# First modulation by channel chunks and eight tiles multiplied as chunks come, in a two-block fp32 transformer kernel

## What is computed

```
mod   = silu(c)     @ ada_w + ada_b        # 1024 -> 6 * 1024
mod_c = silu(c_ctx) @ ada_w + ada_b
sh1, sc1, g1, sh2, sc2, g2 = split(mod, 6);  sh1c, sc1c, ... = split(mod_c, 6)
h  = rms_norm(x,   norm1_w) * (1 + sc1)  + sh1      # 512 tokens
hc = rms_norm(ctx, norm1_w) * (1 + sc1c) + sh1c     # 256 context tokens
p  = h @ w_in                                       # q, k, v, z, xs, b, c, dt
kc, vc, xs_c, b_c = parts of hc @ w_in
```

## Time and profile before

| | us |
|---|---|
| median of 3 runs | 1377.66 |
| lowest, highest | 1375.05, 1383.27 |
| the profiled execution | 1382.15 |
| its span | 1380.4 |
| busy in the span: PE, weight loads, VectorE, ACT, GpSimd | 1320.3, 1068.9, 573.1, 601.8, 619.4 |

### The profile page before, as it was taken

One profiled execution on the slowest core, in us unless ns is written; L12 is line 12 of the kernel. 1 busy time (PEld: TensorE's weight loads), 2 busy tenths in 40 slices (PEclk: granted clock), 3 DMA queues, 4 the chain that ended last, 5 costly groups with the idle time before them and its releaser, 6 DMA issues.

```text
span 1380.4 us, 17922 instructions
## 1 busy us (share of the span) xinstructions
PE 1320.3 (96%) x6626; PEld 1068.9 (77%) x6626; DVE 573.1 (42%) x1123; ACT 601.8 (44%) x937; POOL 619.4 (45%) x507
## 2 busy tenths in 40 slices
PE   8999999998898999999999989999989999999998
PEld 1787878777777788888888778766868888888886
DVE  2577544778446344444522371686330000001123
ACT  3722545874436344443322464687353323223231
POOL 0234334347623544444565734344614444444562
PEclk9999999999999999999999989999999999999999
DMA  9427454040131544545322412110303222232221
GB/s 392 164 101 267 165 163 96 32 153 1 62 122 57 217 182 182 190 190 216 149 108 94 166 61 86 37 47 32 122 18 104 91 91 91 94 109 102 92 92 61
DMA packets 27036, 165.60 MB, mean 120 GB/s; under 512 B 2736, under 2 KB 5040, under 8 KB 8544
## 3 DMA queue, kind: packets, MB, share of 16 engines
q1 hardware_dynamic: 24960, 150.11, 30.3%
q10 hardware_dynamic: 2016, 14.68, 2.9%
HBM read 162.65 MB, written 6.32 MB: 122 GB/s over the span
## 4 chain that ended last, share of the span: by engine, by line
PE 81%; DVE 6%; ACT 4%; POOL 4%; DMA 3%; issue 2%; SPq 0%; ACTq 0%; DVEq 0%; POOLq 0%
PE bank L272 52%; PE bank L331 12%; PE bank L308 6%; DMA ada_ring<-ada_dram 2%; POOL arena L921 2%; PE bank L686 1%; DVE ada_ring L1937 1%; PE bank L1307 1%; PE bank L1279 1%; DMA w_raw<-w_dram 1%; PE bank L525 1%; PE bank L513 1%; POOL arena L923 1%; DVE arena L2002 1%; PE bank L662 1%
## 5 line engine op out<-in xcount | busy, mean ns | idle before, releaser
L265 POOL TENSOR_TENSOR w_lo<-w_raw,w_hi 128x512 fp32r<-128x512 f32 x340 | 462.8, 1393 | 609.7 <-ACT w_hi L256 609.7
L272 PE MATMUL bank<-h_hi,w_hi 128*128 128x512 f32 x1120 | 441.9, 395 | 11.5 <-DVE h_lo L447 6.6
L272 PE MATMUL bank<-h_lo,w_hi 128*128 128x512 f32 x1120 | 438.5, 392 | 0.0
L272 PE MATMUL bank<-h_hi,w_lo 128*128 128x512 f32 x1120 | 438.2, 391 | 0.0
L256 ACT ACTIVATE w_hi<-w_raw 128x2048 fp32r<-128x2048 f32 x88 | 168.6, 1916 | 299.9 <-PE bank L272 176.5
L272 PEld LDWEIGHTS bank<-h_hi,w_hi 128*128 128x128 f32 x1120 | 211.8, 189 | 56.1 <-issue 7.4
L272 PEld LDWEIGHTS bank<-h_hi,w_lo 128*128 128x128 f32 x1120 | 211.9, 189 | 44.8
L272 PEld LDWEIGHTS bank<-h_lo,w_hi 128*128 128x128 f32 x1120 | 212.1, 189 | 42.9
L2266 DVE TENSOR_TENSOR arena<-arena,bank 128x512 f32 (+1 forms) x22 | 15.1, 688 | 209.3 <-PE bank L272 209.3
L2128 DVE TENSOR_TENSOR h_lo<-arena,h_hi 128x1024 fp32r<-128x1024 f32 x22 | 32.4, 1487 | 135.0 <-ACT h_hi L1763 123.5
L1956 DVE SCALAR_TENSOR_TENSOR arena<-bank,params,arena 128x511 f32<-128x511 f32 (+1 forms) x36 | 25.4, 705 | 136.6 <-ACT arena L1743 114.4
(11 more groups left out here) (272 smaller groups left out, 1854.0 us busy)
## 6 DMA issues: line engine op xcount, KB each, us to landing
w_raw<-w_dram SPq DMA_DIRECT2D x92, 1024.0 KB, 4.8
ada_ring<-ada_dram SPq DMA_DIRECT2D x30, 1024.0 KB, 4.8
ada_ring<-ada_dram ACTq DMA_DIRECT2D x14, 1024.0 KB, 5.0
arena<-ada_dram SPq DMA_DIRECT2D x4, 1024.0 KB, 10.7
arena<-x_dram SPq DMA_DIRECT2D x2, 2048.0 KB, 11.6
bias_copies<-bias_rows SPq DMA_DIRECT2D x1, 4096.0 KB, 17.4
arena<-bias_copies SPq DMA_DIRECT2D x4, 768.0 KB, 5.8
out_dram<-arena SPq DMA_DIRECT2D x8, 256.0 KB, 2.1
```

The costliest lines, as they stand in the source:

```text
L265: last = nc.gpsimd.tensor_tensor(w_lo[b % 2][:, part], w_raw[b % 2][:, part], w_hi[b % 2][:, part], ALU.subtract)
L272: last = nc.tensor.matmul(bank[:, :], w[:, ft, k, :], x[:, k, :], start=k == first and m == 0, stop=k == final and m == 2)
```

## The change

The modulation for shift and scale is now made by chunks of 128 channels, and the products start as chunks come.

- `ada1`'s first eight blocks are cut by output channel. Chunks 0 to 3 stay row products on PE (`ada_row_sums`: eight matmuls of 256 columns, 32 output rows each, into four groups of 32 partitions of bank 5; ACT copies the bank; `ada_columns` sums and turns the four groups with a matrix of ones and zeros, `pick`). Chunks 4 to 7 are transposed blocks, and VectorE makes the dots (`lead_dots`), for c and for c_ctx apart.
- PE sums the squares of x itself (32 mean matmuls); VectorE's sums of squares for x and ctx are gone, the latter replaced by one reduction.
- v comes before k in `KINDS`. The first eight tiles (blocks 0 to 3) go to eight banks, `X_BANK`. PE goes through chunks for blocks 0 and 1, then 2, and block 3 at the end; blocks 2 and 3 have their halves in arena space. The context of these eight tiles comes behind all eight, two tiles to a bank.
- v's banks are emptied by ACT between the context's affines; k's ropes stand on VectorE behind the copies of the first four contexts.
- The 16 other modulation blocks: 8 and 9 behind the ropes, then two per tile in n = 8 to 14; ACT issues both loads at the end of its turn n.

The diff, cut to its core:

```diff
-KINDS = [("k", j) for j in range(4)] + [("v", j) for j in range(4)] + [("xs", j) for j in range(4)] \
+KINDS = [("v", j) for j in range(4)] + [("k", j) for j in range(4)] + [("xs", j) for j in range(4)] \
...
+N_LEAD, N_ROW = 8, 4
+DOTS = [(4, 0), (5, 0), (4, 1), (6, 0), (7, 0), (5, 1), (6, 1), (7, 1)]
...
         def load_ada(eng, src, c, off=0):
 
-            eng.wait_ge(ada_used, c - 1 + off)
+            if c < 10:
+                eng.wait_ge(dots_done, N_DOT)
+            else:
+                eng.wait_ge(ada_used, c - 9 + off)
...
+        X_BANK = [0, 1, 2, 3, 6, 7, 4, 5]
...
+            sp.dma_start(con[:], T["con"]).then_inc(con_in, 16)
             load_block(sp, 0)
+            for k in range(4):
+                sp.dma_start(X[:, 2 * k:2 * k + 2, :], T["x"].rearrange("p (c n) -> p c n", c=DC)[:, 2 * k:2 * k + 2, :]).then_inc(x_in[k], 16)
+            load_lead(0)
             load_block(sp, 1)
+            load_lead(1)
+            load_lead(2)
+            load_block(sp, 2)
+            load_lead(3)
+            load_lead(4)
+            sp.dma_start(HC, T["ctx"].rearrange("p (c n) -> p c n", c=DC)).then_inc(ctx_in, 16)
+            for c in range(5, DC):
+                sp.wait_ge(rows_done, c - 4)
+                load_lead(c)
+            load_block(sp, 3)
...
+            def ada_row_sums(c):
+                pe.wait_ge(row_in[c], 16)
+                slab = lead_slot[c].rearrange("p f d -> p (f d)").rearrange("p (k n) -> p k n", k=DC)
+                for k in range(DC):
+                    g = slice(32 * (k % 4), 32 * (k % 4) + 32)
+                    last = nc.tensor.matmul(ps[5][g, 0:256], silu_pad[:, k, :], slab[:, k, :], start=k < 4, stop=k >= 4)
+                last.then_inc(rows_done, 1)
...
+            ada_row_sums(0)
+            ada_columns(0)
+            pe.wait_ge(row1_out, 4)
+            lead_products(0, (0,))
+            ada_row_sums(1)
+            ada_columns(1)
+            lead_products(0, (1,))
+            ada_row_sums(2)
+            ada_columns(2)
+            lead_products(0, (2,))
+            lead_products(1, (0,))
+            ada_row_sums(3)
+            lead_products(1, (1,))
+            ada_columns(3)
+            lead_products(1, (2,))
+            for b in (0, 1):
+                lead_products(b, (3,))
+            lead_products(2, (0, 1, 2, 3))
+            for k in (4, 5, 6, 7):
+                for b in (0, 1, 2):
+                    lead_products(b, (k,))
...
+            pe.wait_ge(lo_done, 4)
+            for ft in (0, 1):
+                if ft == 1:
+                    pe.wait_ge(hctx_scaled, 1)
+                for k in range(DC):
+                    last = chunk_products(3, ft, ps[X_BANK[6 + ft]], k)
+                last.then_inc(half_used, 1)
...
             for n, (kind, j) in enumerate(KINDS):
-                if n == 5:
-                    load_ada(act, T["ada1"][10], 10)
-                if 5 <= n < 15:
-                    c = 2 * n + 1 if n < 9 else n + 9
-                    load_ada(act, T["ada1"][c], c)
...
-                if 5 <= n < 8:
-                    load_ada(act, T["ada1"][2 * n + 2], 2 * n + 2)
+                if N_LEAD <= n < 15:
+                    load_ada(act, T["ada1"][2 * n - 6], 2 * n - 6)
+                    load_ada(act, T["ada1"][2 * n - 5], 2 * n - 5)
...
+            lead_low(3)
+            dve.wait_ge(row1_out, 4)
+            lead_dots(4, 0)
+            lead_xn(5)
+            lead_dots(5, 0)
+            lead_xn(6)
+            lead_low(4)
+            lead_dots(4, 1)
+            lead_xn(7)
+            lead_low(5)
+            lead_dots(6, 0)
+            dve.wait_ge(sq_done, 16)
+            nc.vector.tensor_reduce(ctx_sum, ctx_sq.rearrange("p c n -> p n c"), AX_X, ALU.add).then_inc(sq_used, 8)
+            lead_dots(7, 0)
+            lead_low(6)
+            lead_dots(5, 1)
+            lead_low(7)
+            scale_of(dve, 1)
+            lead_dots(6, 1)
+            dve.wait_ge(scale_out, 2)
+            nc.vector.tensor_tensor(HC, HC, ps[5][:, 0:CTX].unsqueeze(1).to_broadcast([P, DC, CTX]), ALU.mult).then_inc(hctx_scaled, 1)
+            lead_dots(7, 1)
...
+            dve.wait_ge(ctx_done, 4)
+            for n in range(4):
+                nc.vector.tensor_copy(vcT[:, n, :], lead_ctx(n)).then_inc(ctx_free, 1)
+            for n in range(4, N_LEAD):
+                dve.wait_ge(half_used, n + 1)
+                dve.wait_ge(tile_free, n)
+                rope(ps[X_BANK[n]], kT[:, n - 4, :], 1.0)
...
-                if 4 <= n < 8:
-                    add_ada1(2 * n)
-                    add_ada1(2 * n + 1)
-                if 8 <= n < 16:
-                    add_ada1(n + 8)
+                if N_LEAD <= n < 15:
+                    add_ada1(2 * n - 6)
+                    add_ada1(2 * n - 5)
```

More of the change, by code:

```diff
@@ L56 @@
 CCOL, _at = {}, 0
-for _n, _w in [("ident", 128), ("trif", 128), ("trib", 128), ("ones", 128), ("mean", 128), ("mean512", 128), ("eps", 1), ("epseps", 1)]:
+for _n, _w in [("ident", 128), ("trif", 128), ("trib", 128), ("ones", 128), ("mean", 128), ("mean512", 128), ("eps", 1), ("epseps", 1), ("pick", 2)]:
     CCOL[_n] = (_at, _w)
@@ L373, in add_squares @@
                 nc.vector.tensor_tensor(s, s, buf[:, k % 2, 0:n], ALU.add).then_inc(sq_used, 1)
-        def mean(pe, r, buf, bank, n=S):
-            pe.wait_ge(sq_used, 8 * r + 8)
-            s = buf[:, 2, 0:n] if r != 1 else tmp[:, 3, 0:n]
-            for t in range(n // P):
-                last = nc.tensor.matmul(ps[bank][:, t:t + 1], s[:, t * P:(t + 1) * P], con_("mean")[:, 0:1], start=True, stop=True)
-            last.then_inc(mean_done, 1)
         def mean_head(pe, r, buf, bank):
@@ new lines, in _ @@
+            for k in range(DC):
+                pe.wait_ge(sq_done, 2 * (k // 2) + 2)
+                for t in range(4):
+                    last = nc.tensor.matmul(ps[4][:, t:t + 1], tmp[:, k % 4, t * P:(t + 1) * P], con_("mean")[:, 0:1],
+                                            start=k == 0 and t == 0, stop=k == DC - 1 and t == 3)
+                    if k % 2 and t == (2 if k == DC - 1 else 3):
+                        last.then_inc(sq_used, 2)
+            last.then_inc(mean_done, 1)
@@ new lines, in ada_columns @@
+            def ada_columns(c):
+                pe.wait_ge(rows_out, c + 1)
+                if c >= 2:
+                    pe.wait_ge(dots_done, c - 1)
+                for f in range(2):
+                    last = nc.tensor.matmul(ps[6 + c % 2][:, 2 * f:2 * f + 2], ada_rows[c % 2][:, f * P:f * P + P], con_("pick"), start=True, stop=True)
+                last.then_inc(cols_done, 1)
+            ada_row_sums(0)
+            ada_columns(0)
+            pe.wait_ge(row1_out, 4)
+            lead_products(0, (0,))
@@ L1281, in _ @@
                 if k == 5:
-                    pe.wait_ge(con_in, 16)
-                    mean(pe, 0, SQ1, 4)
+                    pe.wait_ge(sq_used, 16)
+                    for t in range(CTX // P):
+                        last = nc.tensor.matmul(ps[5][:, t:t + 1], ctx_sum[:, t * P:(t + 1) * P], con_("mean")[:, 0:1], start=True, stop=True)
+                    last.then_inc(mean_done, 1)
                 if k == 6:
-                    spread(pe, 0, 4).then_inc(scale_out, 1)
-            mean(pe, 1, SQ1, 5, CTX)
@@ L1287, in _ @@
-            pe.wait_ge(row_out, 1)
-            rows = A(A_ACC1, 2048)
-            for f in range(16):
-                last = nc.tensor.transpose(ps[6][:, 2 * f:2 * f + 2], rows[0:2, f * 128:(f + 1) * 128], ident[0:2, 0:2])
-            last.then_inc(modt_done, 1)
-            spread(pe, 1, 5, CTX).then_inc(scale_out, 1)
-            for k in range(DC):
-                last = nc.tensor.matmul(ps[2 + k // 4][:, k % 4 * P:(k % 4 + 1) * P], silu_c[:, k, 0:1].to_broadcast([P, P]), ident,
-                                        start=True, stop=True)
@@ new lines, in lead_ctx_chunk @@
+            def lead_ctx_chunk(n, k, start, stop):
+                hi, lo = halves(n // 2)
+                for m, (w, x) in enumerate(((hi, hc_hi), (hi, hc_lo), (lo, hc_hi))):
+                    last = nc.tensor.matmul(lead_ctx(n), w[:, n % 2, k, :], x[:, k, :], start=start and m == 0, stop=stop and m == 2)
+                return last
+            pe.wait_ge(tile_free, 2)
+            for k in range(DC):
+                pe.wait_ge(hctx_low, k + 1)
+                for n in range(4):
+                    last = lead_ctx_chunk(n, k, k == 0 and n < 2, k == DC - 1 and n >= 2)
```

350 lines of the change are left out of this document (209 added, 141 removed).

## The result

The changed kernel takes 1432.7 us (median of 4 runs, 1427.29 to 1437.71). The kernel before, run beside it, takes 1376.36 (median of 4). The ratio is 1.039, 95% interval 1.036 to 1.042: **slower, by 56 us**. The prediction was 1421, in a range of 1400 to 1443. Its sum, though, was made of one term that came out 18 us too small and one that came out 8 too large, so the experiments had to price both.

A forecast was written before the change was run, and what follows sets the result against it. PE was taken as the bound, busy 96% of 1380.4 us. A start 4 us earlier at tile 8, then long load rounds, made +43 behind tile 16: 1425 against the profiled run, 1421 against the median; range 1400 to 1443.

The forecast's parts named there:

- some 6 us: From 135 to 240 us, PE waits about this long, released by ACT, ahead of each turn group.
- Rival A: Tiles 8 to 14: the modulation loads and dots don't hold PE, the earlier start decides; -15 us, 1363; chance 4%.
- 21 us of earlier start have shrunk to 4: First product at 26.0 instead of 47.28, but tile 8's turn copies end at 134.7 against 138.44 before.
- Means end 18.7: At the start, PE's 16 broadcasts and 32 one-column mean matmuls, 0.25 us each, are done at 18.7 us.
- 6.9 us a chunk: Chunks 0 to 3: sums, copy, small matmuls, modulation, affines, low part and products in series, PE working 3 to 4.
- rival B: A worse start: serial sums +7, low clock in chunks 0 to 3 +5, disturbed dots +4; 1437 us; chance 16%.
- rounds of 15.4 and 17.2: Tiles 8 to 13: load, dots, taps and turn copies take 15.4 us, 17.2 after odd tiles, against PE's 9.25.
- one round, from the end of ACT's turn copies: Tiles 8 to 14: landing 5.0, second block 2.5, dots 2.4, with hand-over 10.0, then 5.33 us to the next copies' end.
- the issue comes 1.0 later: After odd tiles, a high part on ACT stands in front of the modulation loads and delays their issue 1.0 us.
- rival E: Tiles 8 to 14: ACT's queue issues loads past a waiting Silu, rounds 5 us shorter; -35 us, 1386; chance 5%.
- my 0.8: After odd tiles, low parts and a weight block's load meet dots and landing, adding 0.8 us to the round.
- my two signs of failure: Wrong if PE shows no such waits from 135 to 240 us, or tile 8's turn copies end over 15 us from 134.7.

The follow-up runs named there:

- sp_loads: The changed kernel with modulation blocks 10 to 23 loaded by SP as slots come free, not by ACT at the turn's end: 1399.44 us, ratio 1.012.
- old_start: The kernel before, start unchanged, with only the new scheme of two modulation blocks per tile, loaded by ACT at the turn's end: 1416.96 us, ratio 1.027.
- all_ring: The best kernel (1363.30 us) with the modulation loads put back on ACT at the end of turn n: 1403.09 us, ratio 1.017.
- act_early: The changed kernel with ropes ahead of the context copies and ACT's two loads behind the turn's first middle tap: 1393.22 us, ratio 1.009.
- pipe: The changed kernel with SP's loads and ropes first, plus row sums and columns made one chunk ahead of the products: 1378.30 us, ratio 0.999.
- pipe_wide: The changed kernel with SP's loads, ropes first, sums and columns one chunk ahead, and x's means by 512-column matmuls: 1368.93 us, ratio 0.993.
- both: The changed kernel with modulation loads issued by SP and k's ropes ahead of the first context copies: 1388.01 us, ratio 1.006.

## Why the prediction was right, and where it was not

**Right in sign and mechanism.** The rounds of two loads, four dots, taps and SiLU hold PE from tile 9 to 16, and PE can't run ahead of the turn copies; sp_loads, old_start and all_ring each price that at 36 to 39 us at the mark. I had 47 for it (a gain of 4 at tile 8 turned into a loss of 43). VectorE waited 4.7 to 5.2 us for DMA in each of the seven tiles, as forecast. PE's waits of "some 6 us" ahead of each turn group were 7.0 twice, 1.4 and 1.7, and none behind tile 9. Rival A (the ring doesn't hold PE) is out. Its condition, loads in flight early, is what sp_loads and act_early make true, and then PE does keep its pace. My reason against it, that dots and taps alone make 4.8 + 5.3 us a round, was wrong: the 5.3 hold work of ACT that the next dots don't wait for, and with early loads (sp_loads) rounds were 8.1 to 10.3.

**Wrong: "21 us of earlier start have shrunk to 4".** This has the wrong sign: nothing of the earlier start is left at tile 8, it is 14 us behind. I put the end of turn 8's copies at 134.7, against 138.44 before; it was 152.81. By steps, to the taps of tile 8 (129.4 against 147.49, +18.1):
- "Means end 18.7", first product 26.0: it was 24.7 and 33.47, +7.5. The squares came late (PE waited 2.73 for them), and the 32 one-column means took 0.38 us each (12.19 in all) instead of 0.25, at a falling clock.
- "6.9 us a chunk": 8.75, 9.16 and 10.59, +5.6 more up to chunk 3's products at 61.97 instead of 48.9. I had the chain right and its clock wrong: products 2.6 us a chunk, not 1.4, sums 1.94 three times. My sum had slips too: the terms listed make 6.75, not 6.9, and 26.0 and three rounds of 6.9 make 46.7, so 2.2 of the 48.9 stand in no term.
- Chunks 4 to 7: low part 7 at 88.17, 26.2 behind chunk 3's products, against 25.9. The reduction took 3.62, not 2.28; the disturbed dots I had counted.
- From there to tile 8's taps 59.3 instead of 54.6, in part by these: the context's scaling only at 92.33, two rope sums of 1.51 and 1.83 beside GpSimd.

This is rival B by its clock, and not by its serial sums; the measured 1432.7 is nearer to B's 1437 than to my 1421. The row sums I put at 1.7 took 1.07 at the full level and 1.94 at the lower. Eight matmuls at 0.44 one after another would be 3.5, so four column groups gave a factor of 3.3, an estimate. The Trainium skill (TensorE: Matmul & The Clock Gate, the part on packing small matmuls) has 2.38x for three; this trace has more with four.

**Wrong: rounds of 15.4 and 17.2.** They were 13.9 and 16.5; from tile 8's taps to the turn group behind tile 16 the sum was 106.8 instead of 115.0. The failed steps are "one round, from the end of ACT's turn copies" and "the issue comes 1.0 later": I had ACT's queue issue the loads behind the turn copies and the high part. The rows show it at 165.39, 0.2 us **ahead** of the first turn copy and 1.2 ahead of the high part, as soon as the context's SiLU was under way. In all seven turns it comes within 0.1 us of that SiLU's start. That is rival E in small: the issue slips past activations that only stand in line, not past the SiLU that waits. I had misread a row of before: the issue at 147.13 came when it did because the dots of its slot's last block ended just ahead of it, and not because of the high part:

```profile
145.81 1.28 DVE L1937 CUSTOM_DVE_ANT_0 ada_ring<-ada_ring,arena,params 128x1024 f32<-128x1024 f32 x1
```

The disturbance in odd rounds was larger than my 0.8: three of four dots take 1.8 to 2.3 us, +2.6 to +2.9.

The Trainium skill (SBUF — State Buffer, the part on two separate sides) says that a VectorE instruction with two SBUF inputs and a GpSimd one that reads SBUF take turns on a shared pair of ports. The trace agrees: in the ring 1.28 us becomes up to 2.30 only beside GpSimd's low parts, and not beside its fills, which read nothing (1.27 at 206.81).

**So the number stood in part by cancellation**: +18.1 and -8.2 at these two steps, and 2.7 instead of 1 to 2 for the lower clock behind tile 16, give 55.5 where I had 43. The two misses took 10 us off each other; that was luck. Either alone would still have ended inside 1400 to 1443 (1439 and 1413). Of my two signs of failure one came true: tile 8's turn copies ended 18 us from 134.7.

## What to carry to other kernels

Ask of every load where its issue stands in its engine's order, and how much other work lies between it and the first use: the same two loads a tile cost 36 us at the mark behind the SiLU, and issued ahead of it they left PE without a wait at the turn groups. A start that is cut into chunks is a chain through all engines; make each engine's share of chunk c + 1 ahead of the last step of chunk c. Of the edits to the start this gave the most here (10.9 us at the mark). An early first product is worth only what arrives at the next shared wait. Here 14 us earlier at the first product were 14 us later at tile 8, and with ring, ropes, order and means mended the same idea is 1.3% faster than the kernel before: 1363.30 against 1379.17 us, ratio 0.987 (0.984 to 0.989).

## What the runs showed of the hardware

- One-column fp32 matmuls let the clock fall though PE shows no gap: 0.51 from 15 to 20 us in pipe, where the 512-column ones of pipe_wide have 1.00 in the same window. The wait ahead of the means is not the cause: pipe and pipe_wide have one of 2.0 and 2.3 us, and both has none from 5.2 us on and falls all the same. The rows: pipe, pipe_wide, both.

```profile
15.00:20.00 5.00, 5.00 (x26) 5.00 (x26) 0.00 (x0) 1.58 (x2) 1.44 (x2) 0.51 1.00 419
```

```profile
15.00:20.00 5.00, 5.00 (x29) 2.41 (x27) 0.00 (x0) 2.04 (x3) 1.26 (x2) 1.00 1.01 423
```

```profile
16.00:20.00 4.00, 4.00 (x20) 4.00 (x20) 0.00 (x0) 1.06 (x1) 0.00 (x0) 0.50 1.02 424
```

- A reciprocal on VectorE takes 1.70 to 1.77 us for 256 columns, where a product over 512 takes 0.68: about five times as long a column.
- A reduction over a strided 128x2048 takes 3.62 us, a product of the same size 2.28.
- The same instructions put the first product at 31.6 to 34.7 us in one execution each of five kernels, so one trace of a start tells little under about 3 us.
